# Delta rule of a two-block kernel: part of VectorE's elementwise work moved to GpSimd

## The reference

```python
def rwkv7_scan(r, w, k, v, kk, a, reverse):
    def step(state, inp):
        r_t, w_t, k_t, v_t, kk_t, a_t = inp
        sa = jnp.einsum('bhij,bhj->bhi', state, -kk_t)
        state = (state * w_t[:, :, None, :]
                 + sa[..., None] * (kk_t * a_t)[:, :, None, :]
                 + v_t[..., None] * k_t[:, :, None, :])
        return state, jnp.einsum('bhij,bhj->bhi', state, r_t)
...
    y = (rwkv7_scan(r_h, decay[:, :, 0], k_dir[:, :, 0], v_h, kk, a[:, :, 0], False)
         + rwkv7_scan(r_h, decay[:, :, 1], k_dir[:, :, 1], v_h, kk, a[:, :, 1], True))
...
    gates = jax.nn.sigmoid(u[..., RWKV_COLS + DA_COLS:].astype(jnp.float32)).reshape(B, S, N_BRANCH, D)
```

## Time and profile before

| | |
|---|---|
| runs, median (lowest to highest) | 1664.79 us (1664.04 to 1665.77) |
| profiled execution, span from first to last instruction | 1662.5 us |
| PE busy | 1633.7 us (98%) |
| DVE busy | 1059.4 us (64%) |
| ACT busy | 732.1 us (44%) |
| POOL busy | 98.8 us (6%) |
| delta rule's stage, 206 to 470 us: PE, DVE, ACT, POOL busy | 256.59, 214.13, 124.32, 9.72 us |

### The profile page before, as it was taken

The page is one execution under the profiler, slowest core; times in us unless marked ns, Lnnn a source line. Parts: engine busy times, 40 slices in busy tenths (PEclk is TensorE's granted clock), DMA queues, the critical chain, the costliest instruction groups (busy, mean ns, idle before and its releaser), DMA issues. The chain is left out here.

```text
span 1662.5 us, 30282 instructions
## 1 busy us (share of the span) xinstructions
PE 1633.7 (98%) x12906; PEld 1292.8 (78%) x12906; DVE 1059.4 (64%) x1508; ACT 732.1 (44%) x1105; POOL 98.8 (6%) x123
## 2 busy tenths in 40 slices
PE   9999999999999999999999999999999999999997
PEld 6666777777767888888888788886578888888887
DVE  6867589888657577577765773365986654343434
ACT  5444555534265443231324553337775543232323
POOL 0000000000000100001111000031101000000001
PEclk9999999999999999999999999999999999999999
DMA  6212231112145343446563222320002233233321
GB/s 229 85 51 75 83 117 42 41 42 98 36 171 183 127 164 136 156 162 218 192 216 112 86 92 77 114 89 26 20 2 89 86 105 101 90 101 101 101 90 51
DMA packets 51318, 172.81 MB, mean 104 GB/s; under 512 B 6129, under 2 KB 9329, under 8 KB 50417
## 3 DMA queue, kind: packets, MB, share of 16 engines
q1 hardware_dynamic: 41456, 134.71, 24.1%
q0 software_dynamic: 9728, 36.18, 6.5%
HBM read 160.64 MB, written 8.39 MB: 102 GB/s over the span
## 5 line engine op out<-in xcount | busy, mean ns | idle before, releaser
L376 PE MATMUL pair<-h_hi,w_hi 128*128 128x512 f32 x1008 | 402.2, 399 | 1.5 <-DVE w_lo L422 1.0
L378 PE MATMUL pair<-h_hi,w_lo 128*128 128x512 f32 x1008 | 393.0, 390 | 0.0
L377 PE MATMUL pair<-h_lo,w_hi 128*128 128x512 f32 x1008 | 392.9, 390 | 0.0
L422 DVE TENSOR_TENSOR w_lo<-w_raw,w_hi 128x1024 fp32r<-128x1024 f32 (+1 forms) x224 | 265.2, 1188 | 147.7 <-ACT w_hi L401 147.5
L401 ACT CAST w_hi<-w_raw 128x1024 fp32r<-128x1024 f32 (+1 forms) x224 | 220.9, 992 | 229.0 <-PE pair L378 212.1
L376 PEld LDWEIGHTS pair<-h_hi,w_hi 128*128 128x128 f32 x1008 | 189.3, 188 | 55.6 <-issue 16.4
L377 PEld LDWEIGHTS pair<-h_lo,w_hi 128*128 128x128 f32 x1008 | 189.5, 188 | 39.9 <-issue 2.8
L378 PEld LDWEIGHTS pair<-h_hi,w_lo 128*128 128x128 f32 x1008 | 189.3, 188 | 40.2
L376 PE MATMUL pair<-ff_f_hi,w_hi 128*128 128x512 f32 (+1 forms) x536 | 204.3, 381 | 0.6 <-DVE w_lo L422 0.6
L378 PE MATMUL pair<-ff_f_hi,w_lo 128*128 128x512 f32 (+1 forms) x536 | 203.6, 380 | 0.0
L377 PE MATMUL pair<-ff_f_lo,w_hi 128*128 128x512 f32 (+1 forms) x536 | 203.6, 380 | 0.0
(11 more groups left out here) (465 smaller groups left out, 2465.6 us busy)
## 6 DMA issues: line engine op xcount, KB each, us to landing
w_raw<-in_w_ff SPq DMA_DIRECT2D x128, 512.0 KB, 3.3
mod_w<-in_w_mod POOLq DMA_DIRECT2D x48, 512.0 KB, 3.7
w_raw<-in_w_in SPq DMA_DIRECT2D x22, 512.0 KB, 3.4
w_raw<-in_w_gate SPq DMA_DIRECT2D x16, 512.0 KB, 3.3
w_raw<-in_w_out SPq DMA_DIRECT2D x16, 512.0 KB, 3.3
w_raw<-in_w_rwkv SPq DMA_DIRECT2D x15, 512.0 KB, 3.3
w_raw<-in_w_da SPq DMA_DIRECT2D x12, 512.0 KB, 4.6
w_raw<-in_w_ple_gate SPq DMA_DIRECT2D x8, 512.0 KB, 3.3
```

The costliest lines, as they stand in the source:

```text
L376: nc.tensor.matmul(out, w_hi, x_hi, start=(k == 0), stop=False)
L377: nc.tensor.matmul(out, w_hi, x_lo, start=False, stop=False)
L378: last = nc.tensor.matmul(out, w_lo, x_hi, start=False, stop=(k == kt - 1))
L422: nc.vector.tensor_tensor(lo[:, s % SPLIT_SLOTS, 0:cols], pr.raw[:, w % RAW_SLOTS, 0:cols], hi[:, s % SPLIT_SLOTS, 0:cols].bitcast(F32), A ...
```

## The change

Three kinds of work go from VectorE to GpSimd; no other engine's instructions are touched, and PE's stand in the same order.

- The low parts of gate jobs 2 to 15 (jobs 0 and 1 are made before this stage and stay on VectorE). GpSimd makes the low part of j + 2 right behind the DMA issue of job j.
- The four scaled factors of direction 1 of each pair: for the first pair behind point 8 of the preparation, for the others behind point 9 of the pair ahead. The semaphore `scaled` becomes one per direction.
- The sum of a pair's two halves, behind point 5 of the next pair.

```diff
-            if self.low_point(j) == point and j + 2 < self.JOBS:
-                self.low(dve, j + 2)
-
-    def pool(self, pool):
-        for j in range(self.JOBS - 1):
-            pool.wait_ge(self.out, j + 1)
-            pool.dma_start(self.spill[:, j, :], self.staged).then_inc(self.stored, 16)
+
+    def pool(self, pool, point):
+        for j in range(self.JOBS):
+            if self.point_of[j] + 1 == point:
+                if j < self.JOBS - 1:
+                    pool.wait_ge(self.out, j + 1)
+                    pool.dma_start(self.spill[:, j, :], self.staged).then_inc(self.stored, 16)
+                if j + 2 < self.JOBS:
+                    self.low_pool(pool, j + 2)
+
+    def low_pool(self, pool, j):
+        pool.wait_ge(self.hi_made, j + 1)
+        self.pr.nc.gpsimd.tensor_tensor(self.weight_low(j), self.weight(j), self.w_hi[:, j % 2, :].bitcast(F32), ALU.subtract).then_inc(self.lo_made, 1)
...
             @block.gpsimd
             def _(pool):
+                def scaled(p):
+                    a, r = dirs[1][p % 2], U[:, p, :]
+                    pool.wait_ge(s["exps"], 4 * p + 4)
+                    pool.wait_ge(s["bk"], 2 * p + 2)
+                    nc.gpsimd.tensor_tensor(chunks(a["Rt"]), chunks(r), inc(a, 1), ALU.mult).then_inc(s["scaled1"], 1)
+                    nc.gpsimd.tensor_tensor(chunks(a["Kt"]), chunks(kk[:, :]), ex(a, 1), ALU.mult).then_inc(s["scaled1"], 1)
+                    nc.gpsimd.tensor_tensor(a["Kh"], a["sg"], a["pinv"], ALU.mult).then_inc(s["scaled1"], 1)
+                    nc.gpsimd.tensor_tensor(a["Bh"], a["aa"], a["pinv"], ALU.mult).then_inc(s["scaled1"], 1)
+
                 nc.clear_and_free_semaphores(list(earlier.values()))
-                gates.pool(pool)
+                for point in range(gates.start_of_pairs):
+                    gates.pool(pool, point)
+                    if point == 8:
+                        scaled(0)
+                for p, point in enumerate(pair_points):
+                    for i in range(gates.PAIR):
+                        gates.pool(pool, point + i)
+                        if i == 5 and p:
+                            pool.wait_ge(s["yo"], 2 * p)
+                            nc.gpsimd.tensor_tensor(U[:, p - 1, :], U[:, p - 1, :], U[:, 7 + p, :], ALU.add).then_inc(s["ysum"], 1)
+                        if i == 9 and p + 1 < RT:
+                            scaled(p + 1)
...
                     if i % 3 == 0:
-                        pe.wait_ge(s["scaled"], 8 * p + 4 * (1 + i // 3))
+                        pe.wait_ge(s[f"scaled{i // 3}"], 4 * p + 4)
...
-                    scaled(0, 0)
+                    scaled(0)
                     for point in range(7, 11):
                         gates.dve(dve, point)
-                    scaled(0, 1)
+                    dve.wait_ge(s["exps"], 4)
                     ends_across(0)
...
-                        if p:
-                            dve.wait_ge(s["yo"], 2 * p)
-                            nc.vector.tensor_tensor(U[:, p - 1, :], U[:, p - 1, :], U[:, 7 + p, :], ALU.add).then_inc(s["ysum"], 1)
...
                         if more:
-                            for d in range(2):
-                                scaled(p + 1, d)
+                            scaled(p + 1)
+                            dve.wait_ge(s["exps"], 4 * p + 8)
                             ends_across(p + 1)
```

More of the change, by code:

```diff
@@ L1029, in __init__ @@
         self.start_of_pairs = len(self.STEPS) - RT * self.PAIR
-    def low_point(self, j):
-        at, pair = self.point_of[j] + 3, self.point_of[j] + 3 - self.start_of_pairs
-        if pair >= 0 and pair % self.PAIR == 2:
-            return at + (2 if pair // self.PAIR == RT - 1 else 4)
-        return at
     def plan(self):
@@ L1153, in rwkv_block @@
                  "y5", "y64", "mv", "mvout", "n", "nout", "pp", "phiout", "psiout",
-                 "rb", "rbout", "ends", "ysum", "step", "zout", "fixed", "y", "yo", "ksum", "bonus", "bsum", "bout", "scaled", "zero")
+                 "rb", "rbout", "ends", "ysum", "step", "zout", "fixed", "y", "yo", "ksum", "bonus", "bsum", "bout", "scaled0", "scaled1", "zero")
         s = pr.stage_sems("rw_", names)
@@ L1197, in _ @@
                 sp.wait_ge(s["bk"], 2 * RT)
-                sp.wait_ge(s["scaled"], 8 * RT)
+                for d in range(2):
+                    sp.wait_ge(s[f"scaled{d}"], 4 * RT)
                 sp.wait_ge(s["ksum"], RT)
@@ L1483, in squares @@
                     if p:
-                        act.wait_ge(s["scaled"], 8 * p)
+                        for d in range(2):
+                            act.wait_ge(s[f"scaled{d}"], 4 * p)
                         act.wait_ge(s["bk"], 2 * p)
@@ L1524, in exps @@
                     if p:
-                        act.wait_ge(s["scaled"], 8 * p)
+                        for e in range(2):
+                            act.wait_ge(s[f"scaled{e}"], 4 * p)
                     nc.scalar.activation(inc(a, d), chunks(a["cum"]), ACT.Exp, scale=-DECAY_RATE).then_inc(s["exps"], 1)
@@ L1662, in keys, with scaled @@
                         nc.vector.tensor_tensor(a["aa"], kk[:, :], a["aa"], ALU.mult).then_inc(s["bk"], 1)
-                def scaled(p, d):
-                    a, r = dirs[d][p % 2], U[:, p, :]
-                    dve.wait_ge(s["exps"], 4 * p + 2 * d + 2)
-                    dve.wait_ge(s["bk"], 2 * p + d + 1)
-                    nc.vector.tensor_tensor(chunks(a["Rt"]), chunks(r), inc(a, d), ALU.mult).then_inc(s["scaled"], 1)
-                    nc.vector.tensor_tensor(chunks(a["Kt"]), chunks(kk[:, :]), ex(a, d), ALU.mult).then_inc(s["scaled"], 1)
-                    nc.vector.tensor_tensor(a["Kh"], a["sg"], a["pinv"], ALU.mult).then_inc(s["scaled"], 1)
-                    nc.vector.tensor_tensor(a["Bh"], a["aa"], a["pinv"], ALU.mult).then_inc(s["scaled"], 1)
+                def scaled(p):
+                    a, r = dirs[0][p % 2], U[:, p, :]
+                    dve.wait_ge(s["exps"], 4 * p + 2)
+                    dve.wait_ge(s["bk"], 2 * p + 1)
+                    nc.vector.tensor_tensor(chunks(a["Rt"]), chunks(r), inc(a, 0), ALU.mult).then_inc(s["scaled0"], 1)
+                    nc.vector.tensor_tensor(chunks(a["Kt"]), chunks(kk[:, :]), ex(a, 0), ALU.mult).then_inc(s["scaled0"], 1)
+                    nc.vector.tensor_tensor(a["Kh"], a["sg"], a["pinv"], ALU.mult).then_inc(s["scaled0"], 1)
+                    nc.vector.tensor_tensor(a["Bh"], a["aa"], a["pinv"], ALU.mult).then_inc(s["scaled0"], 1)
                 def ends_across(p):
```

## The result

The changed kernel takes 1669.63 us (median of 7 runs, 1667.60 to 1670.92), the one before 1664.79 (7 runs): ratio 1.003, interval 1.002 to 1.004, so 4.8 us slower. The forecast was 1668.5, in a range of 1665.0 to 1672.0. Its profiled execution spans 1667.9 us, 5.4 more than before. Up to the stage PE stands where it stood (0.08 us earlier), at its last gate k-step it is 5.36 us late.

The account below looks back on a forecast made before the run. The prediction took PE as the bound, so that only its waits could change. Its terms, +3.5 + 0.75 - 0.55 = +3.7 us, gave a span of 1666.2 and, with 2.3 from span to median, 1668.5 us (range 1665.0 to 1672.0).

Parts of the forecast that it names:

- Prices: Cost of moved work on GpSimd: a low part 2.38 us, a factor or a sum 1.29.
- the rival of slow forms: GpSimd is slower on the chunked or the wide form: +5.2 us in all, 1670.0; chance 0.10.
- The collision and the start: In the first pair's preparation, VectorE and GpSimd take turns on two-SBUF-operand work; PE's first transposes start at 234.15, not 229.50.
- Low part 2 "costed at nothing": Low part 2, early at the start, adds 0: VectorE then waits for PE's gate job 1 anyway.
- "+3.5": At the start, PE reaches the transposes of direction 1 3.5 us later; bounds +2 to +5.
- "The sum hardly depends on the order": At the start, with VectorE's four factors kept together, GpSimd's chain would end at 236.9 and PE wait there instead.
- "PE comes back slow from its wait": After its 5.4 us wait at the start PE loses 2 us more: 1670.5; chance 0.20.
- "+0.75": In three pairs, a GpSimd low part holds VectorE, making a PE step 0.1 to 0.4 us late: +0.75 us.
- "-0.55": In two pairs, VectorE's fifth-level product, freed of a low part and a sum, ends a PE wait: -0.55 us.
- "Nothing collides there": In a pair, VectorE finishes its two-operand factors by 332.9, before GpSimd's low part and factors, so no turns are taken.
- One-operand work: Rival: GpSimd's low part also holds VectorE's transposes in each of four pairs, +4.4 us more: 1672.9; chance 0.08.
- Side by side: Rival: the engines do not take turns, only GpSimd's latency counts, +1.0 us at the start: 1665.2; chance 0.15.

Follow-up runs that it names:

- e3: The changed kernel, but GpSimd begins low part 3 only when VectorE's four factors of direction 0 are done; ratio to the kernel before 1.0029.
- e4: The changed kernel with the first pair's factors of direction 1 back on VectorE, low parts 2 and 3 still on GpSimd; ratio to the kernel before 1.0009.
- e5: The changed kernel run once more, unaltered; ratio to the kernel before 1.0024.
- e11: Of the change, only the 16 factors of direction 1 move to GpSimd; low parts and sums stay on VectorE; ratio to the kernel before 1.0051.
- e7: Of the change, only the 14 low parts move to GpSimd; factors and sums stay on VectorE; ratio to the kernel before 1.0037.
- e10: The changed kernel plus 16 matmuls that nothing reads, issued on PE ahead of its wait for the first factors; ratio to the kernel before 1.0022.
- e2: The changed kernel plus 24 matmuls that nothing reads, issued on PE ahead of its wait for the first factors; ratio to the kernel before 1.0032.
- e9: As e7, but in three pairs GpSimd begins one low part only when VectorE's two small copies are done; ratio to the kernel before 1.001.
- e1: The changed kernel with low parts 2 and 3 and the first pair's factors of direction 1 back on VectorE; ratio to the kernel before 1.0001.
- e6: As e1, with low part 4 back on VectorE as well; ratio to the kernel before 0.9998.
- e8: Of the change, only the sums of a pair's halves (three additions) move to GpSimd; ratio to the kernel before 0.9998.

## Why the prediction was right, point by point

- **What bounds it**: right. PE's steps decide, VectorE's 18 us less of busy time brought no gain in time, and a pair's window is as full as before (56.46 us of 57; 55.5 was the mark for wrong).
- **Prices**: a low part takes 2.36 to 2.40 us undisturbed (forecast 2.38, extrapolated), `Kh` and `Bh` 1.28 to 1.30, the sum 1.26 (1.29). The two chunked factors take 1.18 and not 1.29; the rival of slow forms falls.
- **The collision and the start**: right in kind. VectorE's and GpSimd's factors take turns; e3, e4, e5 and e11 move the stall as turns would. The turns were 1.6 us, not 1.8, but the order assumed, one factor ahead of low part 3, is that of e5 and not of the first profile. The forecast of 234.15 for PE's first transposes lies between their 233.42 and 235.00.
- **Low part 2 "costed at nothing"**: right while the masks' transfer lands in time. It holds L1673 for 2 us in e3, e5 and e7 too (2.56 us each), and VectorE's first factor starts at 226.87, 226.74 and 226.85 all the same, 226.95 before: the wait for gate job 1 covers it, as the prediction said. In the first profile VectorE had waited 0.67 us for the masks as well, and the two together made the first factor 0.3 us late (227.25), which let low part 3 go first. The prediction had no term for that.
- **"+3.5" for the start**: the term that was mis-sized; it measures +5.7 and, with one factor ahead, +4.8. In that order, the one that the prediction worked out, the turns alone, clock up, are +2.5 (e10: 236.17 against 233.64), an us less than forecast, and the rest of e5's 4.8 is the clock. In the order of the first profile the turns are some +4.1, an estimate (235.00 and e10's 2.77 us), and the clock 1.6.
- **"The sum hardly depends on the order"**: wrong in the traces, by 1.4 to 1.6 us with the clock left out: +2.5 with one factor ahead (e10), +3.9 with GpSimd kept back (e3), some +4.1 with none ahead. In the time no difference can be told.
- **The rival "PE comes back slow from its wait"** (chance 0.20): it came true. It was priced at 2 us from the program's start; at the transposes of direction 1 e5 against e10 gives 2.3. The Trainium skill, in "TensorE: Matmul & The Clock Gate" (Part 1: The HAM clock gate), has an idle PE fall to half clock; the trace agrees, with 0.50. A term for it belonged in the sum, at a chance well above 0.20. As a forecast of the time it isn't clearly the better one: its 1670.5 is 0.9 above the median, 1668.5 is 1.1 below, and e5 is 4.0 us above the kernel before, where the forecast said 3.7 and this rival 5.7; e2 and e10, with the clock up, don't differ from e5 in time.
- **"+0.75" for the pairs**: absent. L1706 is held by 1.0 us (1.66 long, in 0.68 before), not 1.5, because GpSimd comes to its low part 0.5 us sooner than forecast; L1848 still ends 0.5 us ahead of PE's step. **"-0.55"**: there, at 0.33 in each of two pairs. From the start's step to the last gate k-step the changed kernel gains 0.35 us in all where +0.2 was forecast.
- **"Nothing collides there"** in the pairs, with VectorE's lead named as the cover: right, and thin. VectorE's copies end at 339.1 and the low part starts at 339.45. e7 takes away the cover, and 3.3 us of waits appear; e9 puts it back by a wait, and they are gone.
- **One-operand work**: the transposes are not held (0.70 beside a low part), so that rival falls in what it was priced for. But copies and `tensor_scalar` operations with one SBUF tensor are held (2.43 and 2.56 us). The Trainium skill's page "SBUF — State Buffer" (Who interferes with whom) separates them the same way: copy and tensor_scalar can enter two-port modes, which take the ports shared with GpSimd. The trace agrees. The prediction left these two kinds out: it asked only about the transposes.
- **Side by side**: false, as e3 shows and the start's rows do. What GpSimd's slower factors would cost with no turns at all no run shows; the +1.0 of this rival stays an estimate.

That the forecast lay only 1.1 us from the median is in part luck: errors with opposite signs met. With one factor ahead (e5) the forecast had the turns too dear by 1.0 us and the pairs by 0.7, and left out the clock, 2.3. In the first profile's order it had the turns too cheap by about 0.6, the pairs too dear by 0.55, and left out 1.6 of clock. That the loss is made at the start is shown, by e1, and that the two engines take turns there by the rows and by e3, e4 and e11; of the sizes forecast, only the sum is right.

What stays open: the waits of PE without a releaser. Between 206 and 480 us they sum to 0 in e9, 0.3 to 1.1 in most kernels, and 2.0 to 2.5 in e10 and e2, at other matmuls in each. No run tells what places them, and for differences under 1 us between builds they are the limit. No version beats the kernel before by what can be measured; e6 and e8, at 0.9998, come nearest.

## What to carry to other kernels

Before moving elementwise work from VectorE to GpSimd, lay the two engines' instructions side by side in time: where both read two SBUF tensors, or VectorE copies or scales one, each waits out the other's whole instruction, and GpSimd's are twice as long (2.38 us against 1.14 for a low part, 1.18 to 1.30 against 0.60 for a factor). Here such work cost nothing only where VectorE was doing something else (the sums in e8, low parts and factors of the pairs in e6), and even then it gained no time that can be measured. Such a cover has to be made by a wait (e9), not left to chance. And when a change lengthens a wait of PE to several microseconds, count PE's return at the lower clock as part of the price: 1.6 to 2.3 us at the next step here, though little of it came back in the time when it was taken away.

## What the runs showed of the hardware

- **Who gets the turn is not plain alternation.** In e7 GpSimd's low part, issued at 336.62, let VectorE's L1707 (issued later, at 337.03) and L1708 pass at their usual pace of 0.60 and ran when the copies came; in e5, issued at 226.77, it let only the factor pass that VectorE had begun at 226.74, and held the very next one.
- **VectorE can be held across GpSimd's DMA issue, and isn't always.** In e10 VectorE's `key_sum` started when GpSimd's last factor was just over, and was held until the end of the low part behind the issue; in e5 the same instruction started 0.01 us later beside the same issue (235.68), and was not held. What decides that isn't known. VectorE in e10, then in e5:

```profile
235.78 3.44 DVE L1722 TENSOR_TENSOR norm_pair<-x 128x512 f32<-128x512 f32 x1
```

```profile
235.79 0.69 DVE L1706 TENSOR_TENSOR norm_pair<-x 128x512 f32<-128x512 f32 x1
```

And GpSimd in e10:

```profile
235.66 0.58 POOL L1103 DMA_DIRECT2D g_spill<-norm_pair  x1
236.27 2.39 POOL L1109 TENSOR_TENSOR w_raw_low<-w_raw,gate_hi 128x1024 fp32r<-128x1024 f32 x1
```

- **Equal waits, other clocks.** After 2.93 us without a matmul the clock was still 1.00 in e4 and e9, and 0.50 after 2.93 us in e7; after 1.85 us in e3 it was 0.57. Windows of 232 to 234 us, e4 first, then e7:

```profile
232.00:234.00 2.00, 2.00 (x16) 1.82 (x16) 2.00 (x4) 1.35 (x2) 0.56 (x1) 1.00 0.05 20
```

And e7:

```profile
232.00:234.00 2.00, 2.00 (x9) 1.60 (x8) 2.00 (x5) 1.28 (x2) 0.56 (x1) 0.50 0.24 94
```
